# Three norms of a two-block network: the last weight chunk ahead of each computed by column halves, with its squares and column totals taken tile by tile

## The reference

```python
def rms_norm(x, g):
    xf = x.astype(jnp.float32)
    y = xf * lax.rsqrt(jnp.mean(xf * xf, axis=-1, keepdims=True) + EPS)
    return (y * g.astype(jnp.float32)).astype(x.dtype)
...
def modulate(h, shift, scale):
    return h * (1 + scale) + shift
...
def ada_params(cvec, w_ada, b_ada):
    return jnp.split(jax.nn.silu(cvec) @ w_ada + b_ada, N_ADA, axis=-1)
```

## Time and profile before

| | us |
|---|---|
| median of 3 runs | 1607.86 |
| lowest and highest of them | 1606.58 and 1609.05 |
| the profiled execution, its own time | 1609.37 |
| its span from the first to the last instruction | 1606.4 |
| TensorE busy in the span | 1565.8 (97%) |
| VectorE busy | 1029.6 (64%) |
| ScalarE busy | 751.4 (47%) |

### The profile page before, as it was taken

One profiled execution on the slowest core, in us unless ns is written; L12 is line 12 of the kernel. 1 busy time (PEld: TensorE's weight loads), 2 busy tenths in 40 slices (PEclk: granted clock), 3 DMA queues, 4 the chain that ended last, 5 costly groups with the idle time before them and its releaser, 6 DMA issues.

```text
span 1606.4 us, 27446 instructions
## 1 busy us (share of the span) xinstructions
PE 1565.8 (97%) x11374; PEld 1412.3 (88%) x11374; DVE 1029.6 (64%) x1498; ACT 751.4 (47%) x1079; POOL 105.5 (7%) x106
## 2 busy tenths in 40 slices
PE   8999999999999999998999999999999998999998
PEld 6797677887878787978999999999999998999998
DVE  5835746433443436776665668558787889887786
ACT  4214624223232333264444555667564668665554
POOL 0100100000000000000000010201120200020110
PEclk9999999999999999999999999999999999999999
DMA  9861254333242342325445552235555544555551
GB/s 396 325 236 53 117 225 157 104 131 131 104 157 104 131 157 79 132 79 210 161 166 196 183 179 96 95 121 195 184 184 184 184 158 158 184 184 184 184 184 53
DMA packets 36237, 258.81 MB, mean 161 GB/s; under 512 B 4055, under 2 KB 4056, under 8 KB 5168
## 3 DMA queue, kind: packets, MB, share of 16 engines
q1 hardware_dynamic: 29664, 211.85, 36.8%
q0 software_dynamic: 6480, 45.63, 7.4%
HBM read 256.41 MB, written 1.05 MB: 160 GB/s over the span
## 4 chain that ended last, share of the span: by engine, by line
PE 87%; DVE 7%; ACT 3%; issue 2%; DMA 1%; SPq 0%; DVEq 0%; ACTq 0%
PE ps L496 18%; PE ps L497 18%; PE ps L498 18%; PE ps L515 4%; PE ps L517 4%; PE ps L516 4%; PE ps L585 2%; PE ps L586 2%; PE ps L587 2%; PE ps L601 2%; DMA ada_r<-in_w_ada 1%; DVE small L1845 1%; DVE w_lo L1713 1%; PE ps L701 1%; PE ps L725 1%
## 5 line engine op out<-in xcount | busy, mean ns | idle before, releaser
L1213 ACT ACTIVATE w_hi<-w_raw 128x1024 fp32r<-128x1024 f32 x380 | 398.1, 1056 | 547.7 <-PE ps L498 316.8
L1713 DVE TENSOR_TENSOR w_lo<-w_raw,w_hi 128x1024 fp32r<-128x1024 f32 x380 | 466.9, 1233 | 212.7 <-ACT w_hi L1213 209.2
L496 PE MATMUL ps<-h_hi,w_hi 128*128 128x256 f32 (+1 forms) x1584 | 486.7, 307 | 5.8 <-issue 2.8
L497 PE MATMUL ps<-h_lo,w_hi 128*128 128x256 f32 (+1 forms) x1584 | 483.1, 305 | 0.0
L498 PE MATMUL ps<-h_hi,w_lo 128*128 128x256 f32 (+1 forms) x1584 | 483.1, 305 | 0.0
L496 PEld LDWEIGHTS ps<-h_hi,w_hi 128*128 128x128 f32 x1584 | 303.4, 192 | 26.2 <-issue 10.4
L498 PEld LDWEIGHTS ps<-h_hi,w_lo 128*128 128x128 f32 x1584 | 303.3, 192 | 12.8
L497 PEld LDWEIGHTS ps<-h_lo,w_hi 128*128 128x128 f32 x1584 | 303.5, 192 | 12.0
L515 PE MATMUL ps<-g_hi,w_hi 128*128 128x256 f32 (+1 forms) x448 | 140.4, 313 | 0.0
L516 PE MATMUL ps<-g_lo,w_hi 128*128 128x256 f32 (+1 forms) x448 | 140.4, 313 | 0.0
L517 PE MATMUL ps<-g_hi,w_lo 128*128 128x256 f32 (+1 forms) x448 | 140.4, 313 | 0.0
(11 more groups left out here) (353 smaller groups left out, 2303.5 us busy)
## 6 DMA issues: line engine op xcount, KB each, us to landing
w_raw<-in_w_stream SPq DMA_DIRECT2D x190, 1024.0 KB, 4.8
ada_r<-in_w_ada POOLq DMA_DIRECT2D x20, 1024.0 KB, 5.1
ada_g<-in_w_ada POOLq DMA_DIRECT2D x16, 1024.0 KB, 7.5
ada_r<-in_w_ada SPq DMA_DIRECT2D x4, 1024.0 KB, 15.4
ada_g<-in_w_ada SPq DMA_DIRECT2D x4, 1024.0 KB, 26.3
ada_s<-in_w_ada POOLq DMA_DIRECT2D x4, 1024.0 KB, 5.1
x<-in_x_in SPq DMA_DIRECT2D x2, 1024.0 KB, 6.1
pmat<-in_pool_mats POOLq DMA_DIRECT2D x2, 1024.0 KB, 8.3
```

Source lines behind the costliest of these rows:

```text
L496: mm(o, wh, hi[:, k, cols], start=(k == 0), stop=False)
L497: mm(o, wh, lo[:, k, cols], start=False, stop=False)
L1213: A(w_hi[:, n % 2, k, :].rearrange("p k n -> p (k n)"), w_raw[:, n % 4, k.start * CH:k.stop * CH], ACT.Copy)\
L1713: TT(w_lo[:, n % 2, k, :].rearrange("p k n -> p (k n)"), w_raw[:, n % 4, k.start * CH:k.stop * CH], w_hi[:, n % 2, k, :].rearrange("p k n ...
```

## The change

The last chunk ahead of norms 1, 2 and 3 runs in a new `gemm_m`, with m as the outer loop: the first output tile (tile 6 of `x`) is complete after 24 of its 48 matmuls, and `half_done` tells so. `half_used` comes from m = 1, k = 3, the 36th matmul, where it came from the 24th. `gated` waits for each half by itself, `squares` takes tiles 6 and 7 in two activations, and `add_squares(k, 3)`, an addition on VectorE, is gone: TensorE totals the squares of tile 7 by themselves (`tile_sums`), in a PSUM bank for each 128 tokens. The totals of everything up to tile 6 stand ahead of the first `ada_chunk`, those of tile 7 one `ada_chunk` earlier than the totals stood before. In norms 2 and 3 the broadcast stands one `ada_chunk` earlier too, and `rows_at` goes from 0 to 1. In norm 2 `ada_columns` goes out of the gap, to between tile 1 and tile 2 of the next in projection.

```diff
+        SUM_BANK = {1: (0, 1, 4, 5), 2: (0, 1, 4, 5), 3: (4, 5)}
...
+            def gemm_m(n, hi, lo, cols, at=same, bank=None):
+
+                start_chunk(n, at)
+                pe.wait_ge(lo_ready, at(n + 1))
+                s = n % 2
+                bank = 2 * s if bank is None else bank
+                for m in range(2):
+                    for k in range(KT):
+                        o = ps[:, bank + m, 0:cols.stop - cols.start]
+                        wh, wl = w_hi[:, s, k, m * P:(m + 1) * P], w_lo[:, s, k, m * P:(m + 1) * P]
+                        mm(o, wh, hi[:, k, cols], start=(k == 0), stop=False)
+                        mm(o, wh, lo[:, k, cols], start=False, stop=False)
+                        last = mm(o, wl, hi[:, k, cols], start=False, stop=(k == KT - 1))
+                        if m and k == KT // 2 - 1:
+                            last.then_inc(half_used, 1)
+                    last.then_inc((half_done, gemm_done)[m], 1)
...
+                        if k == 2 and c == 0:
+                            ada_columns(10, ADA_GAP[1])
...
+            def tile_sums(k, tile):
+
+                if tile == 6:
+                    pe.wait_ge(sq_used, 3 * k + 3)
+                    pe.wait_ge(sq_tile, k)
+                    parts = (acc2[:, 0], sq[:, 1, 0])
+                else:
+                    pe.wait_ge(sq_done, 4 * k + 4)
+                    parts = (sq[:, 1, 1],)
+                for j, bank in enumerate(SUM_BANK[k]):
+                    for i, part in enumerate(parts):
+                        last = mm(ps[:, bank, 0:1], part[:, j * P:(j + 1) * P], ones[:, 0:1], start=(tile == 6 and i == 0),
+                                  stop=(tile == 7))
+                if tile == 7:
+                    last.then_inc(ss_done, 1)
...
             def norm_gap(k, group, gap, sums_at, broadcast_at):
 
+                tile_sums(k, 6)
                 for i in range(ADA_GAP[gap]):
                     if i == sums_at:
-                        norm_sums(k)
+                        tile_sums(k, 7)
...
-                ada_columns(group, ADA_GAP[gap])
+                if k != 2:
+                    ada_columns(group, ADA_GAP[gap])
...
-                for c in (2, 3):
-                    gemm_f(N_WOUT[l] + c, h_hi, h_lo, width, None, bank=WOUT_BANK[l][c])
+                gemm_f(N_WOUT[l] + 2, h_hi, h_lo, width, None, bank=WOUT_BANK[l][2])
+                gemm_m(N_WOUT[l] + 3, h_hi, h_lo, width, bank=WOUT_BANK[l][3])
                 if l == 0:
-                    norm_gap(1, 5, 0, 3, 5)
+                    norm_gap(1, 5, 0, 2, 5)
                 else:
-                    norm_gap(3, 11, 2, 2, 4)
+                    norm_gap(3, 11, 2, 1, 3)
...
+                        elif c > 5 and l == 0 and c == 7:
+                            gemm_m(n, g_hi, g_lo, width, at)
...
-                    norm_gap(2, 10, 1, 3, 4)
+                    norm_gap(2, 10, 1, 1, 3)
...
+                if j == 3 and 1 <= k <= 3:
+                    for m in range(2):
+                        act.wait_ge(*((x_tile, k), (psum_free, n + 1))[m])
+                        A(sq[:, 1, m, 0:w], x[:, 6 + m, 0:w], ACT.Square).then_inc((sq_tile, sq_done)[m], 1)
+                    return
...
                 for m in range(2):
+                    if halves is not None:
+                        dve.wait_ge(*((half_done, halves), (gemm_done, n + 1))[m])
...
+                    if halves is not None and m == 0:
+                        last.then_inc(x_tile, 1)
...
-                    norm(3, mlp_gain, rows_at=0, rows_done=A_GAP3 + ADA_GAP[2])
+                    norm(3, mlp_gain, rows_at=1, rows_done=A_GAP3 + ADA_GAP[2])
...
-                    norm(2, mixer_gain, rows_at=0, rows_done=A_GAP3)
+                    norm(2, mixer_gain, rows_at=1, rows_done=A_GAP3)
```

More of the change, by code:

```diff
@@ L619, in norm_sums @@
                 if k:
-                    pe.wait_ge(sq_last, k)
+                    pe.wait_ge(sq_last, k - 3)
                 parts = (acc2[:, 0], sq[:, 1, 0])[:2 if k else 1]
@@ L1137, in last_chunk @@
                         last = mm(o, wl, g_hi[:, k, 0:SEQ], start=False, stop=(k == KT - 1))
-                    last.then_inc(last_tile, 1)
+                    last.then_inc(half_done, 1)
             def last_norm():
@@ L1144, in last_norm @@
                     if i:
-                        pe.wait_ge(sums_8, i)
+                        pe.wait_ge(sq_tile, 3 + i)
                     for j in range(2):
@@ L1218, in squares @@
                 w = NORMS[k][3]
-                if n is not None:
+                if n is not None and not (j == 3 and 1 <= k <= 3):
                     act.wait_ge(psum_free, n + 1)
@@ L1250, in norm_root @@
                 act.wait_ge(ss_done, k + 1)
-                A(small[:, S_STD:S_STD + w // P], ps[:, 4, 0:w // P], ACT.Sqrt, bias=sm(S_EPS), scale=1.0 / D)\
-                    .then_inc(std_ready, 1)
+                total, std = ps[:, 4, 0:w // P], small[:, S_STD:S_STD + w // P]
+                if k in (1, 2):
+                    total, std = ps[:, :, 0].rearrange("p (a b) -> p a b", a=2)[:, :, 0:2], std.rearrange("p (a b) -> p a b", a=2)
+                elif k == 3:
+                    total = ps[:, 4:6, 0]
+                A(std, total, ACT.Sqrt, bias=sm(S_EPS), scale=1.0 / D).then_inc(std_ready, 1)
             def norm(k, before=None):
@@ L1920, in attention, with gated @@
                     out_lo(q0 + q)
-            def gated(n, tile0, l, part, at=same, bank=None):
-                dve.wait_ge(gemm_done, at(n + 1))
+            def gated(n, tile0, l, part, at=same, bank=None, halves=None):
+                if halves is None:
+                    dve.wait_ge(gemm_done, at(n + 1))
                 bank = tile0 % 4 if bank is None else bank
                 for m in range(2):
+                    if halves is not None:
+                        dve.wait_ge(*((half_done, halves), (gemm_done, n + 1))[m])
                     for s in range(2 - l):
@@ L2096, in _ @@
                     split_lo(n + 2, parts=(0,))
-                    gated(n, 2 * c, l, 16, bank=WOUT_BANK[l][c])
+                    gated(n, 2 * c, l, 16, bank=WOUT_BANK[l][c], halves=(None, 1 + 5 * l)[c == 3])
                     if c < 3:
                         split_lo(n + 2, parts=(1,))
-                    if c:
+                    if c in (1, 2):
                         add_squares(2 * l + 1, c)
@@ L2146, in quarter @@
                                     add_squares(4, 1)
-                            gated(n, 2 * (c - 4), l, 40, at)
+                            if it is None and l == 0 and c == 7:
+                                gated(n + per * q, 6, l, 40, bank=2 * (n % 2), halves=5)
+                            else:
+                                gated(n, 2 * (c - 4), l, 40, at)
                             if last and c == 7:
@@ L2167, in quarter @@
                             split_lo(m, parts=(0,))
-                        if it is None and c > 4 and l == 0:
+                        if it is None and c in (5, 6) and l == 0:
                             add_squares(2, c - 4)
```

11 lines of the change are left out of this document (6 added, 5 removed).

## The result

The changed kernel takes 1617.43 us (median of 4 executions, 1616.60 to 1619.81) and the kernel before, measured with it, 1608.33: ratio 1.0061 with a 95% interval of 1.0049 to 1.0072. It is about 9 us slower. The forecast was 1607.3 in a range of 1604.3 to 1609.7, so it was wrong in sign and size. The profiled execution took 1616.7 us with a span of 1614.8, against 1609.37 and 1606.4. The experiments ran on several chips, on which the kernel before had medians from 1607.34 to 1609.12 us. Each time is therefore given with its ratio to the kernel before on its own chip, and where two experiments differ by a microsecond or two it is the ratios that are compared.

The account below looks back on a forecast made before the run. TensorE was taken to bound the kernel, with 87% of the chain and busy for 97% of the span. Norms 1 to 3 summed to 0.0 - 1.1 + 0.6 = -0.5 us, clock 0, giving 1607.3 us, range 1604.3 to 1609.7.

Parts of the forecast that it names:

- The delay of `x`: Ahead of norms 1 to 3, later `half_used` delays `w_lo` and tile 6 queued behind it; norm 1 head start 0.34 us.
- the idles forecast as 1.4, 1.0 and 2.0: TensorE idles this many us ahead of the first totals of norms 1, 2 and 3, waiting for tile 6's squares.
- the halves work as meant: Rival: tile 6 is taken while the second half runs, front idles go, -4.9 us in all, 1603.0; chance 0.06.
- the new totals are 8 + 4 matmuls instead of 16: Totals at 512 columns take 0.92 + 0.46 us; at 256 columns, 4 + 2 instead of 8 take 0.46 + 0.23.
- The order's sum in the gaps: At unchanged clock: norm 1 0.0 us, norm 2's first matmul 1.55 us earlier, norm 3 +0.6 us.
- The halved chunks in the first three quarters of the MLP: First MLP: cost nothing, since the delayed `w_lo` ends 0.34 us ahead of the chunk's end.
- Norm 2: the gain: First matmul behind norm 2 comes 1.55 us earlier; moved columns lose 0.45 us, sum -1.1 us.
- The last wait: Norm 2: from the broadcast's end to the first matmul behind the norm, at about 622.1, 3.1 us.
- weighed as about equal and keep 0: Clock falls around norms 1 to 3: 0 us in the sum; one fall more or less is 1.7 us.
- slower: Rival: falls at norm 3's front and another gap slow chunks ahead of broadcasts, +1.7 us each, 1610.8; chance 0.08.
- The prediction's own sign of being wrong: In the profile after: tile 6 squared while the chunk runs, or gap clock figures differing by more than one fall.
- The draw: Clock falls in the trace are a draw between runs, not a property of the order; no size beyond the 0 kept.

Follow-up runs that it names:

- split_behind: The changed kernel with the first half of the next weight split moved behind tiles 6 and 7 of `x` and their squares: 1607.55 us, ratio 0.9999.
- totals_twice: The kernel before with the one-column matmuls of norms 1 to 3 issued twice, the first set unused: 1618.26 us, ratio 1.0049.
- add_early: split_behind with VectorE adding tile 6's squares to the sum mid-chunk, so first totals are 8, 8 and 4 records: 1602.88 us, ratio 0.9971.
- fill: The changed kernel with 3, 2 and 4 dummy matmuls in the idle ahead of the first totals of norms 1, 2 and 3: 1610.85 us, ratio 1.0027.
- before_fill: The kernel before with dummy matmuls in TensorE's idle ahead of the totals of norms 1 to 3 and behind norms 2 and 3: 1608.53 us, ratio 1.0001.
- fill3: The changed kernel with 4 dummy matmuls in TensorE's idle at the front of norm 3 alone: 1618.06 us, ratio 1.0046.
- chunks_first: The changed kernel with the first totals behind one `ada_chunk` in norms 1 and 2 and two in norm 3: 1610.9 us, ratio 1.0013.

## Why the prediction was wrong, point by point

**The delay of `x`: right.** `w_lo` came 2.7, 2.7 and 1.4 us later against the chunk (230.84, 612.40, 752.70), the head start of tile 6 was as small as said, and the idles forecast as 1.4, 1.0 and 2.0 were 1.35, 1.01 and 2.03. That this kept tile 6 from being taken early is shown by split_behind, in which it is squared while the chunk runs. The rival "the halves work as meant" priced it at 4.4 us; it was 4.65 of order, and 10 with the clock.

**The totals: the step that failed first.** The prediction said "the new totals are 8 + 4 matmuls instead of 16". The trace's 16 are records, two for each of the 8 matmuls that `norm_sums` issues at 512 columns; the 8 + 4 of the new code were matmuls, priced with the 0.115 us of a record. In records it is 16 + 8 instead of 16. They took 1.94 + 0.98 us at norm 1, not 0.92 + 0.46, 1.5 too little there, 1.4 at norm 2 (its second set priced at norm 1's 0.98) and 0.8 at norm 3 (0.95 + 0.54 against 0.69), 3.8 us in all. The order's sum in the gaps, forecast at 0.0 - 1.55 + 0.6 = -0.95, was +2.8. This one count turns one into the other. The kernel before gave it: 8 matmuls in its `norm_sums` against the 16 records of the rows. The rest of the sum held: norm 1 came out 0.2 under its forecast with this count put right, norm 2 0.1 under and norm 3 0.2 over. The halved chunks in the first three quarters of the MLP cost nothing, as said: from gap 1 to gap 2 it takes 365.91 us before and 365.92 changed. I counted one side in rows and the other in the source. totals_twice and add_early measure the term.

**Norm 2: the gain was there only on paper.** With the totals of 2.8 us the broadcast stands 10.33 us behind the start of the chunk's last matmul, where the forecast had 5.85 and before 7.26. The slow clock is 2.9 of it (the three rows ahead of the broadcast take 1.45, 1.87 and 3.64 us, and 1.07, 1.05 and 1.94 in the profiles without a fall), which leaves 7.4. The last wait (2.12 us, forecast as 3.1 from the broadcast's end) was as said.

**The clock: "weighed as about equal and keep 0".** This is the second step that failed: kept at 0, it was 5.1 us in the gaps and about 3.6 net of the falls that lay behind them before. It was wrong in two ways. The light stretches were not as short as forecast, since the totals in them were twice as long. And I compared only how many stretches there were and not what stands behind them. In the kernel before the chunks ahead of the totals keep TensorE busy, and two of its three falls lie behind the gap, one of them on a first chunk where VectorE sets the pace and where it cost the 0.4 us above. In the changed kernel they lie on the conditioning chunks ahead of the broadcast, with the whole norm queued behind. The rival "slower" had this mechanism and place; it priced two more falls at 3.4 us, gave them 0.08, and put them on an order of -0.5. With the order at +2.8 and the falls at 5.1 the same rival gives 1607.9 + 7.9 = 1615.8, near the 1617.4. The prediction's own sign of being wrong, clock figures of the gaps that differ by more than one fall, came: they differ by three.

**The draw.** The Trainium skill (TensorE: Matmul & The Clock Gate, Part 1) has the count of slow matmuls at the start of a kernel differ between executions. The traces show the same in the middle of one: in five profiles with the changed order at norm 1 the clock took 1.72, 3.45, 5.10, 3.47 and, with dummies in the idle, 0 us. But I used the rule to excuse a zero in the sum. What an order sets is how much there is to draw: at norm 2 that order lost 3.42 us in all four profiles without dummies there, and the median of the changed kernel came out at 1617.4 twice. Beyond that which falls an execution draws stays open.

**The range.** Its upper end held one fall more and norm 3 at its worst, and it took the rest of the order's sum as exact. A factor of two in one counted term was outside it.

## What to carry to other kernels

When a new duration is made from an old row, count both sides in the same unit, the trace's records or the source's instructions, and check the one against the other on the code before. A wait moved to the front of a stretch on the engine that bounds the kernel should be priced with the clock on what stands behind it, since taking 4.4 us of wait away here (split_behind) gave back 4.65 us of order and 5.1 of clock. And a result made early helps only if its consumer's queue is free to take it: the halving was worth nothing until the split stood behind it, and the fewer totals saved nothing until then.

## What the runs showed of the hardware

One-column fp32 matmuls stand as two records each, 0.115 us apart with a weight load for each, and 40 more of them, with no idle added, made three gaps 7.0 us longer instead of 4.6, with a broadcast at 1.2 GHz behind them (2.08 us instead of 1.12). A fall on two conditioning chunks ahead of a broadcast cost 1.6 us (3.54 instead of 1.94), and one on a chunk where VectorE sets the pace 0.4 (197.35 against 196.95). Dummy matmuls in idle time can be worth time (fill: 4.3 to 6.6 us) and can be worth none (before_fill, where the clock fell behind the first of norm 2's and the others ran at 1.2 GHz). What decides in which of several light stretches the clock falls in one execution stays open: fill3 and chunks_first, with their falls in other places or in two groups of times, show that it differs and not why.
